# A recurrent block's output product: its rounded input waits for its own semaphore, and GpSimd forms two half rests

## The chip, the cores and the metric

The kernel runs on one core of one Trainium2 chip. The metric is the device time of one execution in microseconds (us), lower is better. Five engines work side by side, each in its own program order, and meet only through semaphores: TensorE (PE, matrix products), VectorE (DVE), ScalarE (ACT), GpSimd (POOL) and SyncE (SP, which here issues the loads of weights).

## What is computed

A stack of three layers over 256 tokens of width 1024, all in fp32: a mixer of four branches with a feed-forward layer, a gated linear recurrence (HGRN2) with a feed-forward layer, and a gated convolutional recurrence (RG-LRU) with a feed-forward layer. The change lies in the third, between the recurrence and its output product:

```python
def rglru_mixer(h, w_in, conv_w, conv_b, wa, ba, wx, bx, lam, w_out):
    proj = h @ w_in
    y, u = jnp.split(proj, [LRU_WIDTH], axis=-1)
    y = jax.nn.gelu(y.astype(jnp.float32))
    ...                                        # uc: a causal convolution of u; r, ig: two sigmoid gates of uc
    a = jnp.exp(log_a)
    b_in = jnp.sqrt(-jnp.expm1(2.0 * log_a)) * (ig * uc)
    _, hs = lax.associative_scan(combine, (a, b_in), axis=1)
    return (hs * y).astype(h.dtype) @ w_out    # the output product

x = x + mix
x = x + swiglu_2(rmsnorm_2(x, norm_ffn[l]), ffn_w_in[l], ffn_w_out[l])
```

## The kernel before

**Products in three passes.** Each fp32 matrix is split in two: a rounded part (`whi`, `ch`, `hh`: type fp32r) and a rest (`wlo`, `cl`, `hl`: the difference to the rounded part). A product is the sum of rounded by rounded (L527 for tokens as rows, L507 for columns), rounded by rest of the weights (L531, L510), and rest by rounded weights (L535, L515).

**Units of weights.** All weights come in units of 128 x 2048 elements through three slots (NS = 3). For each half of a unit: SP loads it into `raw` (L2207), ACT rounds it into `whi` (L981), DVE forms `wlo = raw - whi` (L1385). Where `on_pool` says so, GpSimd forms the rest of the unit's second half instead (L2006, the same subtraction). `light` (L301) is the list of units for which it does, so far most units of the three feed-forward layers. SP may load a half of unit j+3 once the rest of that half of unit j is set, and ACT may round it once TensorE has read unit j.

**The stretch of the change.** The recurrence's input units for y are `ly` 0 to 3, the units of its output weights `lo` 0 to 3 (each two k rows of 128 by 1024 columns, one k row to a half), and then come `g` 0, `u` 0, `g` 1 and so on of the last feed-forward layer. For the four pairs of channels n, called pair 0 to 3 here, the order written out by hand is:

- DVE scales y out of the PSUM bank (`y_of`, L1432), runs the scan (`scan`, L1933 and L1935), multiplies by the GELU (`gated`, L1942), and forms the rest `cl` (`gated_rest`, L1947), with the rests of weights (L1385) between. From 913.78 us on: y_of(2), gated(0), scan(2), gated_rest(0), gated(1), y_of(3), scan(3), gated_rest(1), rests of `lo` 1, gated(2), gated(3), gated_rest(2), gated_rest(3), rests of `lo` 2 and `lo` 3.
- ACT takes the GELU (L1330), rounds the gated output into `ch` (L1335, which raises `s_uch`), and rounds weights (L981) between: `lo` 1, gelu(2), ch of pair 0, ch of pair 1, gelu(3), `lo` 2, ch of pairs 2 and 3, `lo` 3.
- `cl` raises `s_hs`. DVE's `gated_rest(n)` waits for `s_uch`, so `cl` of a pair always comes after its `ch`.
- TensorE runs `add_product(("lo",), ...)` (L966): unit 0 for both column halves, then units 1, 2, 3 for the first half, then units 1, 2, 3 for the second. For each token half it runs two products of each pass: `ch` by `whi` (L527), `ch` by `wlo` (L531), `cl` by `whi` (L535). Before the first pass it waits for `hi(k)`, before the third for `lo(k)`. Both are `s_hs` so far, though the first two passes read only `ch`.
- GpSimd has nothing in this stretch before the change. Its program reaches the rests of a unit two units ahead, so its first instruction here waits only for `whi`.

```python
        def on_pool(j, h):
            return h == 1 and any(u0 <= j < u1 for u0, u1 in light)
...
                if 0 in parts:
                    for i, k in enumerate(ks):
                        tq.wait_ge(*hi_set(j, i // half_k))
                        tq.wait_ge(*hi(k))
```

Of the kernel before, what the change touches and what calls it, by code (L numbers as in the profile page):

```python
# [74 lines left out]
def build(nc, a):  # L75
    V, A, G, T, S = nc.vector, nc.scalar, nc.gpsimd, nc.tensor, nc.sync
    vq, aq, gq, tq, sq = Waits(V), Waits(A), Waits(G), Waits(T), Waits(S)
    with ExitStack() as root:
        def sem(name):
            return root.enter_context(nc.semaphore(name))  # L80

        def sbuf(ctx, name, shape, dt=f32):
            return ctx.enter_context(nc.sbuf_tensor(name, shape, dt))
# [73 lines left out]
        ch = sbuf(lr, "ch", [128, 8, 256], f32r)  # L157
        cl = sbuf(lr, "cl", [128, 8, 256], f32r)
# [51 lines left out]
        unit_at = {}  # L210
# [87 lines left out]
            raw_value.append(loads[j % NS])  # L298


        light = [(unit_at["g", f, 0] + 2, unit_at["g", f, 0] + 31) for f in range(3)]  # L301

        def on_pool(j, h):
            return h == 1 and any(u0 <= j < u1 for u0, u1 in light)
# [38 lines left out]
        s_pad, s_uch, s_gw = sem("pad_set"), sem("ch_set"), sem("gate_weights_landed")  # L343
# [3 lines left out]
        s_gel, s_gy, s_hs = sem("gelu_set"), sem("gated_set"), sem("lru_out_set")  # L347
# [7 lines left out]
        def turn(key, b, fills=1):  # L355
            fills_of[b] += fills
            turns[key] = (b, evacuations[b], fills_of[b])
            evacuations[b] += 1
            return b

        def free(key):
            b, n, _ = turns[key]
            return s_evac[b], n
# [120 lines left out]
        def halves_of(by_token):  # L484
            return [[(s, i) if by_token else (i, s) for i in range(2)] for s in range(2)]


        def tensor_program():
# [29 lines left out]
            def moving(out, j, t, xh, xl, ks, c0, n, hi, lo, first=True, last=True, parts=(0, 1, 2)):  # L518

                wh, wl = whole(whi, j), whole(wlo, j)  # L520
                r, c = slice(128 * t, 128 * t + 128), slice(c0, c0 + n)
                half_k = units[j][1] // 2
# [4 lines that stand above are left out]
                        tok = T.matmul(out, xh[:, k, r], wh[:, i, c], start=first and i == 0, stop=False)  # L527
                if 1 in parts:
                    for i, k in enumerate(ks):
                        tq.wait_ge(*lo_set(j, i // half_k))  # L530
                        tok = T.matmul(out, xh[:, k, r], wl[:, i, c], start=False, stop=False)  # L531
                if 2 in parts:
                    for i, k in enumerate(ks):
                        tq.wait_ge(*lo(k))
                        tok = T.matmul(out, xl[:, k, r], wh[:, i, c], start=False, stop=last and i == len(ks) - 1)  # L535
                return tok
# [31 lines left out]
            def transposes(c, e):  # L568

                for n in range(2):  # L570
                    b = turn(("tr", e, 2 * c + n), 4 + 2 * n + c)
                    for k in range(2):
                        for t in range(2):
                            col = 512 * c + 256 * n + 128 * k
                            tq.wait_ge(*hn_set(e, 2 * c + t))
                            tq.wait_ge(*free(("tr", e, 2 * c + n)))
                            tok = T.transpose(banks[b][:, 256 * k + 128 * t:256 * k + 128 * t + 128], hn[:, t, col:col + 128], ident[:, :])  # L577
                    tok.then_inc(s_full[b], 1)
# [27 lines left out]
            def add_product(key, n_units, xh, xl, hi, lo, e, by_token=False, inside_second=None, rests_last=False):  # L606

                halves = halves_of(by_token)

                def part(n, s, parts=(0, 1, 2), between=None):  # L610
                    j = unit_at[(*key, n)]
                    for t, c in halves[s]:
                        b, name = 4 + 2 * t + c, ("add", e, t, c)
                        if n == 0 and 0 in parts:
                            turn(name, b, n_units if b == 7 else 1)
                            tq.wait_ge(*free(name))
                        tok = moving(banks[b][:, :], j, t, xh, xl, [2 * n, 2 * n + 1], 512 * c, 512, hi, lo,
                                     first=n == 0, last=n == n_units - 1, parts=parts)
                        if 2 in parts and (b == 7 or n == n_units - 1):
                            tok.then_inc(s_full[b], 1)  # L620
                        if between is not None and (t, c) == halves[s][0]:
                            between()
                    if s == 1 and 2 in parts:
                        used[j, 0] = used[j, 1] = (s_full[7], turns["add", e, 1, 1][2] - n_units + n + 1)

                for n in range(n_units - 3):
                    for parts in ((0, 1), (2,)) if rests_last else ((0, 1, 2),):
                        part(n, 0, parts)
                        part(n, 1, parts)
                for n in range(n_units - 3, n_units):  # L630
                    part(n, 0, between=inside_second if n == n_units - 3 else None)
                for t, c in halves[0]:
                    turn(("sq", e, t, c), 4 + 2 * t + c, 0)
                for n in range(n_units - 3, n_units):
                    if n == n_units - 1 and e != 8:
                        transposes(0, e)
                    part(n, 1)
                for t, c in halves[1]:
                    turn(("sq", e, t, c), 4 + 2 * t + c, 0)
# [207 lines left out]
            def feed_forward(f, e, e2):  # L847
                project_pair([("g", f, 0), ("u", f, 0)], e)
                for j in range(1, 11):
                    project_columns(("g", f, j), e)  # L850
                    project_columns(("u", f, j), e)
                gh, gl = ffn[f][0:2]
                add_product(("down", f), 11, gh, gl, lambda k: (s_gh, 11 * f + k // 2 + 1), lambda k: (s_gl, 11 * f + k // 2 + 1),
                            e2, e2 == 8)
# [108 lines left out]
            project_columns(("ly", 2), 6)  # L963
            project_columns(("ly", 3), 6)
            rot_banks[0] = [0, 1, 2, 3]
            add_product(("lo",), 4, ch, cl, lambda k: (s_hs, k // 2 + 1), lambda k: (s_hs, k // 2 + 1), 7)  # L966
            feed_forward(2, 7, 8)


# [1226 lines left out]
        def sync_program():  # L2196
# [39 lines left out]
            sq.wait_ge(s_u, 16)  # L2236

        tensor_program()
        scalar_program()
        vector_program()  # L2240
# [30 lines left out]
```

## Time and profile before

| | |
|---|---|
| time, median of three runs | 1134.25 us (1134.21 to 1134.31) |
| span of the profiled execution | 1133.1 us |
| PE busy in it | 1119.1 us, 99% |
| DVE, ACT, POOL busy | 659.1, 571.9, 292.8 us |
| granted TensorE clock, mean | 0.999 of full speed |

The span runs from the first to the last instruction of the program, so 1.15 us of the median lie outside it. Times in the profile count from the span's start. A timeline row gives start, length, engine, line, operation, what is written from what, its shape, how often, and in brackets how long the engine had been idle before it and whose work ended that. On DVE and ACT an instruction's record begins up to 0.1 us before the one ahead of it ends, so a train of them is read by its starts.

### The profile page before, as it was taken

The numbers are of one execution on the slowest core, as the hardware profiler recorded it, in microseconds if no ns is written. First come the engines' busy times: TensorE is split into PE (matmuls) and PEld (weight loads), VectorE is DVE, ScalarE is ACT, GpSimd is POOL, SyncE is SP. The second block draws the span as 40 slices with busy tenths as digits, with TensorE's granted clock in tenths as the row PEclk, the third lists the DMA queues.
The fourth block names the chain that finished last, engine by engine and source line by source line (L and its number), as shares of the span: only waits on it lengthen the run. The fifth ranks groups of instructions, "written<-read, shape, count | busy, mean of one in ns | idle before, by whom it ended". The sixth has DMA issues, their size and how long they took to land.

```text
span 1133.1 us, 19238 instructions
## 1 busy us (share of the span) xinstructions
PE 1119.1 (99%) x8085; PEld 1040.8 (92%) x8085; DVE 659.1 (58%) x1052; ACT 571.9 (50%) x866; POOL 292.8 (26%) x193
## 2 busy tenths in 40 slices
PE   8999999999999999999999999999999999999997
PEld 7899989999989999889998889999889989999986
DVE  6755755677666454328897575443237897434324
ACT  6646555555445554336642544444335855544432
POOL 2023100000005445522411205444420003444440
PEclk9999999999999999999999999999999999999999
DMA  8689474544657656664545348665555255666551
GB/s 266 204 252 335 139 238 147 160 151 143 195 159 209 200 170 206 202 200 139 170 125 178 113 152 273 211 190 192 193 184 184 97 181 154 215 191 189 190 183 38
DMA packets 155088, 207.25 MB, mean 183 GB/s; under 512 B 9471, under 2 KB 128409, under 8 KB 155002
## 3 DMA queue, kind: packets, MB, share of 16 engines
q1 hardware_dynamic: 151274, 193.11, 54.4%
q0 software_dynamic: 3728, 12.92, 3.4%
q8 instruction: 64, 1.05, 0.4%
q14 instruction: 22, 0.18, 0.0%
HBM read 204.78 MB, written 4.24 MB: 184 GB/s over the span
## 4 chain that ended last, share of the span: by engine, by line
PE 84%; DVE 11%; ACT 3%; issue 1%; DMA 0%; POOL 0%; SPq 0%; DVEq 0%; ACTq 0%
PE bank L507 17%; PE bank L515 17%; PE bank L510 17%; PE bank L535 9%; PE bank L531 9%; PE bank L527 9%; DVE wlo L1385 4%; PE bank L886 1%; PE bank L802 1%; PE bank L812 1%; ACT whi L981 1%; DVE area L1533 1%; PE bank L577 1%; PE bank L824 1%; DVE uc L1533 0%
## 5 line engine op out<-in xcount | busy, mean ns | idle before, releaser
L1385 DVE TENSOR_TENSOR wlo<-raw,whi 128x1024 fp32r<-128x1024 f32 x275 | 336.5, 1251 | 231.4 <-ACT whi L981 230.6
L981 ACT ACTIVATE whi<-raw 128x1024 fp32r<-128x1024 f32 x362 | 360.4, 1044 | 107.3 <-PE bank L535 100.9
L2006 POOL TENSOR_TENSOR wlo<-raw,whi 128x1024 fp32r<-128x1024 f32 x87 | 222.7, 2560 | 250.9 <-ACT whi L981 250.9
L507 PE MATMUL bank<-hh,whi 128*128 128x256 f32 x1784 | 285.3, 281 | 0.0
L510 PE MATMUL bank<-hh,wlo 128*128 128x256 f32 x1784 | 281.3, 279 | 0.0
L515 PE MATMUL bank<-hl,whi 128*128 128x256 f32 x1784 | 281.3, 279 | 0.0
L507 PEld LDWEIGHTS bank<-hh,whi 128*128 128x128 f32 x1784 | 240.5, 188 | 3.4 <-issue 2.7
L510 PEld LDWEIGHTS bank<-hh,wlo 128*128 128x128 f32 x1784 | 239.8, 188 | 0.0
L515 PEld LDWEIGHTS bank<-hl,whi 128*128 128x128 f32 x1784 | 239.8, 188 | 0.0
L2013 POOL TENSOR_TENSOR st<-st,half 128x1 f32<-128x1 f32 x18 | 10.7, 604 | 331.4 <-DVE st L1402 302.2
L527 PE MATMUL bank<-whi,gh 128*128 128x512 f32 x264 | 81.6, 390 | 0.0
L531 PE MATMUL bank<-wlo,gh 128*128 128x512 f32 x264 | 81.3, 389 | 0.0
L535 PE MATMUL bank<-whi,gl 128*128 128x512 f32 x264 | 81.3, 389 | 0.0
L1211 ACT ACTIVATE sg<-sg 128x512 f32<-128x512 f32 x33 | 20.9, 633 | 94.2 <-DVE sg L1432 94.2
L1215 ACT ACTIVATE gh<-sg 128x512 fp32r<-128x512 f32 x33 | 20.8, 631 | 84.1 <-DVE sg L1765 84.1
L531 PEld LDWEIGHTS bank<-wlo,gh 128*128 128x128 f32 x264 | 49.6, 188 | 10.4
L535 PEld LDWEIGHTS bank<-whi,gl 128*128 128x128 f32 x264 | 49.6, 188 | 10.3
L527 PEld LDWEIGHTS bank<-whi,gh 128*128 128x128 f32 x264 | 49.2, 188 | 9.9
L1765 DVE TENSOR_TENSOR sg<-sg,bank 128x512 f32<-128x512 f32 x33 | 22.7, 688 | 55.6 <-PE bank L515 53.5
L1432 DVE TENSOR_TENSOR sg<-bank,bc_f 128x512 f32<-128x512 f32 x33 | 22.8, 690 | 45.4 <-PE bank L515 45.4
L1006 ACT ACTIVATE bank<-x_sb 128x512 f32<-128x512 f32 x26 | 15.6, 600 | 57.7 <-DVE x_sb L1454 29.9
L1767 DVE TENSOR_TENSOR gl<-sg,gh 128x512 fp32r<-128x512 f32 x33 | 30.7, 931 | 23.3 <-ACT gh L1215 23.3
(318 smaller groups left out, 1217.2 us busy)
## 6 DMA issues: line engine op xcount, KB each, us to landing
raw<-in_ffn_w_in SPq DMA_DIRECT2D x88, 512.0 KB, 3.8
raw<-in_w_in SPq DMA_DIRECT2D x72, 512.0 KB, 4.8
raw<-in_ffn_w_out SPq DMA_DIRECT2D x44, 512.0 KB, 3.2
raw<-in_hgrn_w_in SPq DMA_DIRECT2D x32, 512.0 KB, 4.4
raw<-in_w_ffn_gate SPq DMA_DIRECT2D x22, 512.0 KB, 4.6
raw<-in_w_ffn_up SPq DMA_DIRECT2D x22, 512.0 KB, 4.3
raw<-in_w_ffn_down SPq DMA_DIRECT2D x22, 512.0 KB, 3.4
raw<-in_w_branch SPq DMA_DIRECT2D x16, 512.0 KB, 4.3
```

Source lines behind the costliest of these rows:

```text
L507: T.matmul(out, wh[:, i, c], xh[:, k, :], start=first and (i, k) == pairs[0], stop=False)
L510: T.matmul(out, wl[:, i, c], xh[:, k, :], start=False, stop=False)
L515: t = T.matmul(out, wh[:, i, c], xl[:, k, :], start=False, stop=last and (i, k) == pairs[-1])
L527: tok = T.matmul(out, xh[:, k, r], wh[:, i, c], start=first and i == 0, stop=False)
L531: tok = T.matmul(out, xh[:, k, r], wl[:, i, c], start=False, stop=False)
L535: tok = T.matmul(out, xl[:, k, r], wh[:, i, c], start=False, stop=last and i == len(ks) - 1)
L981: A.activation(half_of(whi, j, h), half_of(raw, j, h), ACT.Copy).then_inc(s_hi[j % NS][h], 1)
L1385: V.tensor_tensor(half_of(wlo, j, h), half_of(raw, j, h), half_of(whi, j, h).bitcast(f32), ALU.subtract).then_inc(s_lo[j % NS][h], 1)
L1432: V.tensor_tensor(dst, two(bank_of("col", *key)[:, :]), bc[:, :].rearrange("p (o t) -> p o t", o=1).broadcast_to([128, 2, 256]), ALU.mult) ...
L1765: V.tensor_tensor(s, s, bank_of("col", "u", f, j)[:, :], ALU.mult).then_inc(evacuated("col", "u", f, j), 1)
L1767: V.tensor_tensor(gl[:, 2 * j:2 * j + 2, :], two(s), gh[:, 2 * j:2 * j + 2, :].bitcast(f32), ALU.subtract).then_inc(s_gl, 1)
L2006: G.tensor_tensor(half_of(wlo, j, 1), half_of(raw, j, 1), half_of(whi, j, 1).bitcast(f32), ALU.subtract).then_inc(s_lo[j % NS][1], 1)
```

## The change

It adds one stretch to `light`: units `lo` 1 and `lo` 2, whose second halves' rests GpSimd then forms instead of DVE. And it gives `add_product` of `lo` the semaphore of `ch`, `s_uch`, for the passes that read `ch`; the third pass keeps `s_hs`. Nothing is computed otherwise than before.

```diff
@@ -298,7 +298,7 @@
-        light = [(unit_at["g", f, 0] + 2, unit_at["g", f, 0] + 31) for f in range(3)]
+        light = [(unit_at["g", f, 0] + 2, unit_at["g", f, 0] + 31) for f in range(3)] + [(unit_at["lo", 1], unit_at["lo", 3])]
 
         def on_pool(j, h):
             return h == 1 and any(u0 <= j < u1 for u0, u1 in light)
@@ -963,7 +963,7 @@
             rot_banks[0] = [0, 1, 2, 3]
-            add_product(("lo",), 4, ch, cl, lambda k: (s_hs, k // 2 + 1), lambda k: (s_hs, k // 2 + 1), 7)
+            add_product(("lo",), 4, ch, cl, lambda k: (s_uch, k // 2 + 1), lambda k: (s_hs, k // 2 + 1), 7)
             feed_forward(2, 7, 8)
```

## Rows read from the trace of the kernel before

**Rows 1.** The page, busy time, share of span and instructions of each engine.

```profile
PE 1119.1 (99%) x8085; PEld 1040.8 (92%) x8085; DVE 659.1 (58%) x1052; ACT 571.9 (50%) x866; POOL 292.8 (26%) x193
```

**Rows 2.** Waits of PE: who for whom, us in total, times, longest.

```profile
PE bank L531 <- DVE wlo L1385: 1.6, 3, 0.7
...
PE bank L527 <- DVE cl L1947: 0.6, 1, 0.6
```

**Rows 3.** Windows: stretch, length, then busy us of PE, PEld, DVE, ACT, POOL.

```profile
942.50:1126.90 184.40, 184.40 (x1333) 173.88 (x1331) 77.29 (x86) 80.46 (x98) 74.94 (x32) 1.00 0.54 171
```

**Rows 4.** Timeline of PE in the output product.

```profile
917.70 0.70 PE L527 MATMUL bank<-whi,ch 128*128 128x512 f32 x2 [0.60 <-DVE cl L1947]
...
918.71 0.62 PE L535 MATMUL bank<-whi,cl 128*128 128x512 f32 x2
...
925.99 0.61 PE L527 MATMUL bank<-whi,ch 128*128 128x512 f32 x2
...
927.31 0.49 PE L531 MATMUL bank<-wlo,ch 128*128 128x512 f32 x1 [0.71 <-DVE wlo L1385]
...
928.44 0.50 PE L531 MATMUL bank<-wlo,ch 128*128 128x512 f32 x1 [0.64 <-DVE wlo L1385]
...
928.78 0.62 PE L535 MATMUL bank<-whi,cl 128*128 128x512 f32 x2
...
929.24 0.63 PE L527 MATMUL bank<-whi,ch 128*128 128x512 f32 x2
```

**Rows 5.** Timeline of DVE in the same stretch.

```profile
914.38 0.68 DVE L1942 TENSOR_TENSOR yg<-yg,ig 128x512 f32<-128x512 f32 x1
...
918.08 0.68 DVE L1432 TENSOR_TENSOR yg<-bank,bc_lr 128x512 f32<-128x512 f32 x1
...
921.17 1.22 DVE L1385 TENSOR_TENSOR wlo<-raw,whi 128x1024 fp32r<-128x1024 f32 x1
...
923.44 1.29 DVE L1942 TENSOR_TENSOR yg<-yg,ig 128x512 f32<-128x512 f32 x2
...
924.82 1.30 DVE L1947 TENSOR_TENSOR cl<-yg,ch 128x512 fp32r<-128x512 f32 x2
...
926.03 1.22 DVE L1385 TENSOR_TENSOR wlo<-raw,whi 128x1024 fp32r<-128x1024 f32 x1
...
927.17 1.22 DVE L1385 TENSOR_TENSOR wlo<-raw,whi 128x1024 fp32r<-128x1024 f32 x1
```

**Rows 6.** Timeline of ACT there: second halves of lo 1, lo 2, then ch.

```profile
913.12 1.05 ACT L981 ACTIVATE whi<-raw 128x1024 fp32r<-128x1024 f32 x1
...
920.28 1.05 ACT L981 ACTIVATE whi<-raw 128x1024 fp32r<-128x1024 f32 x1
...
924.15 1.24 ACT L1335 ACTIVATE ch<-yg 128x512 fp32r<-128x512 f32 x2 [2.83 <-DVE yg L1942]
```

**Rows 7.** Timelines of ACT, POOL and DVE in the first feed-forward layer.

```profile
416.99 1.04 ACT L981 ACTIVATE whi<-raw 128x1024 fp32r<-128x1024 f32 x1
...
418.11 2.40 POOL L2006 TENSOR_TENSOR wlo<-raw,whi 128x1024 fp32r<-128x1024 f32 x1 [3.11 <-ACT whi L981]
...
418.19 3.41 DVE L1385 TENSOR_TENSOR wlo<-raw,whi 128x1024 fp32r<-128x1024 f32 x1
...
349.59 5.21 POOL L2006 TENSOR_TENSOR wlo<-raw,whi 128x1024 fp32r<-128x1024 f32 x2 [4.43 <-ACT whi L981]
...
350.07 2.49 DVE L1767 TENSOR_TENSOR gl<-sg,gh 128x512 fp32r<-128x512 f32 x1 [0.77 <-ACT gh L1215]
352.48 3.41 DVE L1385 TENSOR_TENSOR wlo<-raw,whi 128x1024 fp32r<-128x1024 f32 x1
...
362.61 3.33 POOL L2006 TENSOR_TENSOR wlo<-raw,whi 128x1024 fp32r<-128x1024 f32 x1 [0.97 <-ACT whi L981]
...
364.38 0.69 DVE L1432 TENSOR_TENSOR sg<-bank,bc_f 128x512 f32<-128x512 f32 x1 [0.70 <-PE bank L515]
```

**Rows 8.** Loads from 915 to 945 us: count, size, median us to landing.

```profile
raw<-in_ffn_w_in SPq DMA_DIRECT2D x9, 512.0 KB, 4.7
```

## The prediction

> **What bounds the kernel now.** I read the busy times first: TensorE works 99% of the span [rows 1], so a change can matter only where TensorE waits or is made to wait. The list of its waits comes next. In the stretch of the change it has one wait of 0.60 us for `cl` and two, 0.71 and 0.64 us, for rests of weights [rows 2, 4]. The timeline gives them their place: 917.70, when the output product begins, and 927.31 and 928.44, the two `ch` by `wlo` products of unit `lo` 2 [rows 4]. From 942.50 to 1126.90 PE is busy for all of 184.40 us [rows 3], so what the output product gains or loses reaches the end in full. What sets the three waits is DVE: its train of instructions from gated(0) at 914.38 to the second rest of `lo` 2 at 927.17 has hardly a gap [rows 5]. So the question is what the change does to that train.
>
> **What GpSimd's instruction does to DVE.** The feed-forward layers have such pairs already. The rest on POOL took 2.40 us from 418.11 to 420.51; the same subtraction on DVE, queued at 418.19, lasted 3.41 us instead of 1.22, to 421.60, that is 1.09 us past POOL's end [rows 5, 7]. The 512-wide gl, which reads sg and gh and so nothing that POOL touches, stretched to 2.49 us and ended at 352.56, taking 2.40 us for the hold about 0.56 us after POOL's first of two [rows 7]. So a DVE instruction with two operands in SBUF stands still until POOL's is over. I count ten such starts inside a hold in the three layers, and none that went through. An instruction that reads a PSUM bank does go through: 0.69 us at 364.38, inside POOL's 362.61 to 365.94 [rows 7]. And POOL, when it comes second, waits for the running DVE instruction and then gets in ahead of DVE's next: its second rest ended at 354.80, 2.24 us after gl, and the DVE instruction queued behind gl waited for that (352.48, 3.41 us) [rows 7]. In DVE's train here, gated, scan, gated_rest and the rests have both operands in SBUF; only y_of reads a bank.
>
> **Part one, the wait for `ch`.** It removes up to 0.60 us at 917.70. By itself I price it at nothing: TensorE then reaches the rests of `lo` 2 0.60 us sooner, and DVE delivers them no sooner, so the waits at 927.31 and 928.44 grow by as much. The cover is those two waits; if part two took them away, the 0.60 us would count.
>
> **Part two, two rests to GpSimd.** It takes two DVE instructions of 1.14 us each (step from start to start, 927.17 less 926.03 [rows 5]) off the train and puts two POOL instructions of 2.40 us beside it.
>
> *First hold.* ACT's `whi` of the second half of `lo` 1 ends at 914.17 [rows 6]. POOL follows ACT by 0.08 us (418.03 to 418.11 [rows 7]), so it starts at 914.25, in front of gated(0) at 914.38 [rows 5]; at 418 a lead of 0.08 us was enough [rows 7]. It holds until 916.65. gated(0) ends 0.56 us later, at 917.21, where it ended at 915.06: 2.15 us late, and all behind it, `ch` and `cl` of pair 0 among them. TensorE's output product then begins at about 917.9 on `ch`, and waits again for `cl`, to about 919.75 against 918.71 [rows 4].
>
> *Second hold.* y_of(3) at 918.08 is in the train [rows 5], gelu(3) waits for it and ACT's `whi` of `lo` 2 stands behind gelu(3), so its end moves from 921.33 [rows 6] to 923.48 and POOL is ready at 923.56. DVE has begun the first rest of `lo` 1 at 923.32 (921.17 and 2.15 [rows 5]); it ends at 924.54, POOL gets in and is done 2.24 us later, at 926.78. gated(2), next on DVE with the second rest gone, ends at 927.34 instead of 924.12 (923.44 and 0.68 [rows 5]): 3.22 us late. As a sum: 2.15, plus 2.21 for the second hold, less 1.14 saved. `ch` of pair 2 follows on ACT and gated_rest(2) on DVE, with no slack in either direction (924.15, 924.82 [rows 5, 6]), so the first rest of `lo` 2 ends at 927.25 and 3.22, that is 930.47. The second comes from POOL, long since.
>
> *TensorE.* It stands before that rest from about 928.6. It resumed 0.05 us after DVE's end in the kernel before (928.39, 928.44), took 0.34 us to its next start (928.78), and 0.23 us for a step in flow (929.24 less 928.78, by two) [rows 4, 5]. So 930.52 for the first `wlo` product, 930.86 for the second, 931.09 for the `cl` product that stood at 928.78: **2.3 us late**.
>
> *What is late next: nothing.* `lo` 3's rests follow on DVE, ending at 931.6 and 932.75; TensorE wants them 0.46 us into `lo` 3, at about 933.4 and 933.6. SP's loads queue behind the rests: the first half of `g` 0 leaves at 924.5 instead of 922.4, that of `u` 0 at 930.5 instead of 927.3, and with 4.7 us to land [rows 8] they are there by 929.3 and 935.3, before ACT's turn at about 938.6 and 941.3 (which TensorE's reading of `lo` 1 and `lo` 2 sets). POOL's next work is the normaliser's power at 945 us. So 2.3 us stay, on the profiled span 1133.1 to 1135.4, on the median 1134.25 to **1136.5 us**.
>
> The GPSIMD Engine Reference of the Trainium skill (§ 2.1) puts the floor of a two-input instruction at about 2.5 cycles per element and § 1 the clock at 1.2 GHz; for 1024 elements that is an estimate of 2.13 us, against 2.40 us in the rows. By it each hold would be 0.27 us shorter and the loss about 1.8 us; the measured 2.40 us stands.
>
> **Bounds on what is not shown.** No row has POOL's rest beside gated or a scan, but gl is the same kind of instruction in the same shape. If DVE is first at 914.38, gated(0) goes through, POOL ends at 917.30 and scan(2) takes the blow: 2.2 us instead of 2.15, and 2.36 at the end. If POOL wins the second race too, the loss is 2.6. If POOL has to wait until DVE's queue leaves a gap, it gets in after gated(3), ends at 927.98, and the first rest of `lo` 2 ends at 930.28: 2.1 us. So 2.1 to 2.6 us, and I take 2.3, the row order.
>
> **Rivals.** *The train isn't held up (not slower).* If the stall were of the weights' subtraction alone, or POOL's rest slid beside the recurrence, DVE's train would be 1.14 us early from 922.3 on. TensorE would begin at 917.10, find `ch` ready, want the first rest of `lo` 2 at 925.84 and get it at 926.17 (926.12 and 0.05); the `cl` product would stand at 926.75 against 928.78, a gain of 2.0 us: 1132.2 us, within 0.2% by a little. It decides at 914.38: does gated(0) end at 915.06? Against it speaks gl, held without sharing a tile with POOL [rows 7].
>
> *One hold only.* If the first is as worked out and the second finds DVE between instructions of little weight, gated(2) is 1.0 us late (2.15 less 1.14), the first rest of `lo` 2 ends at 928.25, TensorE's `cl` product stands at 928.9, and the loss is 0.1 us: 1134.4 us. It needs POOL at 923.56 to miss the train; against it, DVE has no gap there [rows 5].
>
> The Trainium skill, SBUF — State Buffer (§ SBUF: two separate sides), has the pair of ports that DVE and GpSimd share as an exclusive lock, held for the whole instruction by the one that starts first. By that rule DVE couldn't keep it over several instructions, which speaks against a late entry of POOL; the row at 352.48 agrees.
>
> **How the numbers follow.** Holds as worked out, with their orders: 0.88, at 2.1 to 2.6 us. One hold: 0.05. No hold: 0.05. Something not seen, such as a longer restart of TensorE: 0.02. This kernel's measurement can tell about 0.2%, 2.27 us, from no change, and my forecast lies just beyond that line, so the main case is split: of 0.88 I give 0.50 to a loss over 2.27 us (2.3, 2.36 and 2.6 lie there, if barely) and 0.38 to less. One hold goes to the same; of no hold, 0.02 to faster. Faster 0.02, same 0.46, slower 0.52. The range takes the bounds 2.1 and 2.6 with 0.5 us on either side for the estimates: 1135.8 to 1137.4 us.
>
> **What would show it.** In the changed profile, POOL's two rests near 914.25 and 924.5; gated(0) and gated(2) of 2.8 and 2.9 us instead of 0.68; TensorE's waits of about 0.9 us for `ch`, 0.6 for `cl`, 1.0 for `ch` of pair 2 and 1.9 for the rest of `lo` 2; the first `cl` product of `lo` 2 at 931.1; no wait of TensorE from 945 us on. A gated(0) of 0.7 us would prove the prediction wrong at its first step, a rest of `lo` 2 before 929.5 at its second.

## The result and the profile after

| | before | changed |
|---|---|---|
| time, median | 1134.25 us (1134.09 to 1134.76, 7 runs) | 1136.98 us (1136.43 to 1138.79, 7 runs) |
| ratio to before | | 1.0028 [1.0019, 1.0037] |
| span of the profiled execution | 1133.1 us | 1135.6 us |
| PE, DVE, POOL busy in it | 1119.1, 659.1, 292.8 us | 1118.9, 660.9, 297.7 us |

The change loses 2.7 us by the medians, a quotient of 1.0024. The seven times aren't one heap: four lie at 1136.43 to 1136.98 us and three at 1138.44 to 1138.79 us. The three draw the mean, 1137.55 us, above the median, and the ratio of 1.0028 is nearer to the quotient of the means. The profiled execution, 1136.83 us, is of the lower group. The upper one is the subject of the last experiments.

GpSimd's two rests in the changed kernel's timeline of POOL:

```profile
914.49 2.40 POOL L2006 TENSOR_TENSOR wlo<-raw,whi 128x1024 fp32r<-128x1024 f32 x1 [52.92 <-ACT whi L981]
923.77 3.24 POOL L2006 TENSOR_TENSOR wlo<-raw,whi 128x1024 fp32r<-128x1024 f32 x1 [6.88 <-ACT whi L981]
```

DVE's train beside them, in the timeline of DVE:

```profile
914.02 0.69 DVE L1432 TENSOR_TENSOR yg<-bank,bc_lr 128x512 f32<-128x512 f32 x1
914.62 2.81 DVE L1942 TENSOR_TENSOR yg<-yg,ig 128x512 f32<-128x512 f32 x1
...
923.54 1.22 DVE L1385 TENSOR_TENSOR wlo<-raw,whi 128x1024 fp32r<-128x1024 f32 x1
924.68 2.89 DVE L1942 TENSOR_TENSOR yg<-yg,ig 128x512 f32<-128x512 f32 x1
...
929.48 1.22 DVE L1385 TENSOR_TENSOR wlo<-raw,whi 128x1024 fp32r<-128x1024 f32 x1
```

The two 512-wide gated products, 0.68 us before [rows 5], take 2.81 and 2.89 us: each lasts until about 0.55 us after POOL's end (914.62 and 2.81 is 917.43, POOL ends at 916.89; 927.57 against 927.01). In the second race DVE was first, with the rest at 923.54; it ended at 924.76, and POOL 2.25 us after it.

TensorE's waits in its timeline, where [rows 4] had 0.60, 0.71 and 0.64 us:

```profile
918.25 0.70 PE L527 MATMUL bank<-whi,ch 128*128 128x512 f32 x2 [1.10 <-ACT ch L1335]
...
919.99 0.73 PE L535 MATMUL bank<-whi,cl 128*128 128x512 f32 x2 [0.58 <-DVE cl L1947]
...
928.37 0.70 PE L527 MATMUL bank<-whi,ch 128*128 128x512 f32 x2 [0.83 <-ACT ch L1335]
930.75 0.73 PE L531 MATMUL bank<-wlo,ch 128*128 128x512 f32 x2 [1.67 <-DVE wlo L1385]
931.32 0.63 PE L535 MATMUL bank<-whi,cl 128*128 128x512 f32 x2
```

And the rest of the kernel, in windows (stretch, length, busy us of PE, PEld, DVE, ACT, POOL, then the granted clock, DMA share and GB/s):

```profile
926.90:930.60 3.70, 1.34 (x5) 0.48 (x3) 3.61 (x5) 3.00 (x4) 0.12 (x1) 1.00 0.64 224
...
945.20:1129.00 183.80, 183.80 (x1331) 173.59 (x1330) 77.12 (x85) 80.02 (x97) 74.95 (x32) 1.00 0.54 171
```

PE never stands from 945.20 on, so what is lost by 931 us reaches the end. The first `cl` product of `lo` 2 starts at 931.32 against 928.78 [rows 4], 2.54 us later. Of these, 0.24 us are an offset that stood on DVE already ahead of GpSimd's first rest (y_of(2) at 914.02 against 913.78 us in the kernel before); an offset of about 0.3 us is there from the first layer on, far ahead of the change. So 2.30 us are the change's.

### The profile page after: what moved, and what is told of

Same layout as the page of the kernel before. It is cut to its first block, busy times and chain, and to the rows that moved or that the text cites. A ratio compares the mean times of both kernels' runs of the same rounds, so it can differ in the third digit from the quotient of the medians.

```text
span 1135.6 us, 19238 instructions
## 1 busy us (share of the span) xinstructions
PE 1118.9 (99%) x8085; PEld 1040.2 (92%) x8085; DVE 660.9 (58%) x1050; ACT 571.7 (50%) x866; POOL 297.7 (26%) x195
## 4 chain that ended last, share of the span: by engine, by line
PE 83%; DVE 11%; ACT 3%; issue 1%; DMA 1%; POOL 0%; SPq 0%; DVEq 0%; ACTq 0%
PE bank L507 17%; PE bank L515 17%; PE bank L510 17%; PE bank L531 9%; PE bank L535 9%; PE bank L527 9%; DVE wlo L1385 3%; PE bank L886 1%; PE bank L802 1%; ACT whi L981 1%; PE bank L812 1%; DVE area L1533 1%; DMA raw<-in_w_in 1%; PE bank L824 1%; PE bank L577 1%
## 5 line engine op out<-in xcount | busy, mean ns | idle before, releaser
L2006 POOL TENSOR_TENSOR wlo<-raw,whi 128x1024 fp32r<-128x1024 f32 x89 | 228.3, 2565 | 310.7 <-ACT whi L981 310.7
```

Source lines behind the costliest of these rows:

```text
L2006: G.tensor_tensor(half_of(wlo, j, 1), half_of(raw, j, 1), half_of(whi, j, 1).bitcast(f32), ALU.subtract).then_inc(s_lo[j % NS][1], 1)
```

## The experiments

Two theories were put to the test first: that the loss comes from DVE standing during POOL's instruction, and, against it, that it comes from the wait or from the order of the rests. Later a third question came up, the upper group. The kernel before ran beside each: its medians were 1134.20 to 1134.35 us.

**One part alone.** First only the wait:

```diff
-            add_product(("lo",), 4, ch, cl, lambda k: (s_hs, k // 2 + 1), lambda k: (s_hs, k // 2 + 1), 7)
+            add_product(("lo",), 4, ch, cl, lambda k: (s_uch, k // 2 + 1), lambda k: (s_hs, k // 2 + 1), 7)
```

> Only the wait for the rounded output's own semaphore; no rest goes to GpSimd. Theory of the hold (GpSimd's subtraction keeps VectorE's two-input instructions standing, VectorE's train sets the end): no change, 1134.2 us within 0.2 us. TensorE begins the output product 0.6 us sooner (wait of 0.60 us gone) and waits 0.6 us longer before the first rest of unit 2. Rival (TensorE's early start and its extra waits are what costs): 1135 to 1136 us, TensorE's products after a wait slower than 0.34 us to the next start, or a granted clock under 1.00 behind them.

Measured: 1134.46 us (11 runs, 1134.15 to 1135.81), ratio 1.0003 [0.9994, 1.0012]. Its timeline of PE, and the row of PE's waits for rests (us in total, times, longest):

```profile
917.00 0.62 PE L527 MATMUL bank<-whi,ch 128*128 128x512 f32 x2
...
923.87 0.50 PE L531 MATMUL bank<-wlo,ch 128*128 128x512 f32 x1 [0.45 <-DVE wlo L1385]
927.60 0.49 PE L531 MATMUL bank<-wlo,ch 128*128 128x512 f32 x1 [0.90 <-DVE wlo L1385]
928.73 0.50 PE L531 MATMUL bank<-wlo,ch 128*128 128x512 f32 x1 [0.64 <-DVE wlo L1385]
```

```profile
PE bank L531 <- DVE wlo L1385: 2.2, 4, 0.9
```

The output product begins 0.70 us earlier than in [rows 4], without a wait, and the gain is gone by 928.73. Its waits for rests add up to 2.2 us, as much as the 1.6 us for rests and the 0.6 us for `cl` of [rows 2] together: a wait of 0.45 us for the rest of `lo` 1 is new, and the first for `lo` 2 is longer, 0.90 us against 0.71. The 0.26 us by which its median lies above the kernel before beside it is within the noise. Part one is worth nothing by itself, as priced.

Then only the rests on GpSimd:

```diff
-        light = [(unit_at["g", f, 0] + 2, unit_at["g", f, 0] + 31) for f in range(3)]
+        light = [(unit_at["g", f, 0] + 2, unit_at["g", f, 0] + 31) for f in range(3)] + [(unit_at["lo", 1], unit_at["lo", 3])]
```

> Only the two rests to GpSimd; the first two passes wait for the rests of the output, as before. Theory of the hold: the same loss as the whole change, 2.3 us (1136.5 us), since TensorE stands before the first rest of unit 2 whenever it began; gated of pair 0 and of pair 2 held 2.8 to 2.9 us. Rival (the early start costs): no more than 0.5 us of loss here. Rival (an extra loss outside the output product, seen in the runs of the change near 1138.6 us, belongs to the hold): some runs near 1138.5 here too, and none with the wait alone.

Measured: 1136.63 us (11 runs, 1136.37 to 1138.13), ratio 1.0022 [1.0014, 1.0031]. The loss of the lower group is all in part two. One of the 11 times, 1138.13 us, stands apart; the profiled execution was that one, and it shows something new. Its timeline and windows of PE:

```profile
920.61 1.19 PE L527 MATMUL bank<-whi,ch 128*128 128x512 f32 x2 [2.96 <-DVE cl L1947]
921.60 1.05 PE L531 MATMUL bank<-wlo,ch 128*128 128x512 f32 x2
922.46 1.05 PE L535 MATMUL bank<-whi,cl 128*128 128x512 f32 x2
...
926.69 0.63 PE L531 MATMUL bank<-wlo,ch 128*128 128x512 f32 x2
```

```profile
923.00:926.00 3.00, 3.00 (x9) 2.32 (x8) 3.00 (x4) 1.24 (x2) 1.69 (x1) 0.50 0.00 0
```

After one wait of 2.96 us (the changed kernel has it in two pieces, 1.10 and 0.58 us) the granted clock is 0.50, that is 1.2 of 2.4 GHz, and two products take 0.86 us from start to start instead of 0.46 until about 926.7. About half of what sets this execution apart is an offset (y_of(2) stands at 914.56 against 913.78 us in the kernel before); by the first `cl` product of `lo` 2, at 932.62 us, about 0.8 us beyond the hold's 2.3 are left for the low clock.

**The changed kernel again**, unaltered, to see whether its two groups come back.

> The changed kernel once more, for the spread of its runs: the seven timed so far lie at 1136.4 to 1137.0 and at 1138.4 to 1138.8 us, the kernel before at 1134.1 to 1134.8. Theory: 1136.5 us is the stall of 2.3 us alone, and the upper group is a second thing; if it is a lower granted clock behind TensorE's long waits, a profile from the upper group shows windows under 1.00 after 930 us and an output product as in the first profile. If it is another order at the port, the output product itself ends 2 us later.

Measured: four runs at 1136.44 to 1136.60 us, four at 1138.25 to 1138.46 us; median 1137.42 us, ratio 1.0028 [1.0018, 1.0038]. The profile, of a run at 1136.60 us, has a low clock too, in another place:

```profile
919.60:924.00 4.40, 4.28 (x12) 3.36 (x13) 4.37 (x8) 3.13 (x4) 0.50 (x1) 0.61 0.00 0
```

It follows the waits of 1.14 and 0.57 us at 917.98 and 919.72, and it costs nothing: TensorE reaches the rest of `lo` 2 later, and waits 1.12 us for it instead of 1.67 us. A clock that falls ahead of a wait is paid out of the wait. The upper group therefore needs a fall behind the last wait.

**One hold at a time**, with the new wait in both; the edits are against the changed kernel. The first, `lo` 1 alone:

```diff
-        light = [(unit_at["g", f, 0] + 2, unit_at["g", f, 0] + 31) for f in range(3)] + [(unit_at["lo", 1], unit_at["lo", 3])]
+        light = [(unit_at["g", f, 0] + 2, unit_at["g", f, 0] + 31) for f in range(3)] + [(unit_at["lo", 1], unit_at["lo", 2])]
```

> The change with only unit 1's second rest on GpSimd; unit 2's stays on VectorE. Theory of the hold, from the train of the kernel before: one hold of 2.15 us less one rest of 1.14 us, so the second rest of unit 2 ends at 929.40 instead of 928.39 and TensorE's first product of the third pass of unit 2 stands at 929.8: 1.0 us late, 1135.3 us. TensorE's waits stay under 1 us each, so if long waits bring the lower clock, no run lies 1.5 us above the rest. Rival (a hold costs nothing once TensorE's own waits are hidden): 1134.3 us.

Measured: 1135.36 us (10 runs, 1135.12 to 1135.91), ratio 1.0009 [0.9999, 1.0018]. DVE in it:

```profile
914.22 2.81 DVE L1942 TENSOR_TENSOR yg<-yg,ig 128x512 f32<-128x512 f32 x1
...
924.26 1.28 DVE L1942 TENSOR_TENSOR yg<-yg,ig 128x512 f32<-128x512 f32 x2
```

gated(0) pays 2.15 us for the hold, the train gets back 1.14 us for the rest it needn't form, and 1.0 us arrives at the end. The interval of the ratio just takes in 1, so this rests on the trace: the first `cl` product of `lo` 2 stands at 929.61 us against 928.78, and y_of(2) at 913.62 against 913.78, which makes 0.99 us. No execution lies 1.5 us above the rest.

The second, `lo` 2 alone:

```diff
-        light = [(unit_at["g", f, 0] + 2, unit_at["g", f, 0] + 31) for f in range(3)] + [(unit_at["lo", 1], unit_at["lo", 3])]
+        light = [(unit_at["g", f, 0] + 2, unit_at["g", f, 0] + 31) for f in range(3)] + [(unit_at["lo", 2], unit_at["lo", 3])]
```

> The change with only unit 2's second rest on GpSimd; unit 1's stays on VectorE. Theory of the hold: GpSimd is ready at 921.4, gets in behind unit 1's first rest at 922.4 and keeps unit 1's second rest standing to 925.7 (3.4 us instead of 1.2). TensorE waits 2.5 us for that and 1.1 us for the first rest of unit 2 at 929.5; the first product of the third pass of unit 2 stands at 930.1: 1.3 us late, 1135.5 us. If a long wait brings the lower clock, some or all runs show it behind the 2.5 us wait, where the 1.1 us wait can take up part of it.

Measured: 1135.81 us (10 runs, 1135.39 to 1136.15), ratio 1.0012 [1.0003, 1.0021]. DVE, then PE, then PE's window:

```profile
921.02 4.52 DVE L1385 TENSOR_TENSOR wlo<-raw,whi 128x1024 fp32r<-128x1024 f32 x2
```

```profile
925.59 0.79 PE L531 MATMUL bank<-wlo,ch 128*128 128x512 f32 x1 [2.49 <-DVE wlo L1385]
```

```profile
926.00:931.00 5.00, 5.00 (x17) 3.97 (x17) 4.91 (x7) 3.13 (x4) 0.00 (x0) 0.70 0.44 121
```

Here POOL lands on the two rests of `lo` 1, which take 4.52 us together instead of 2.35. Behind a single wait of 2.49 us the granted clock is low, as in the run with the rests alone. The time is 0.3 us over the estimate of the hold.

**The hold without the rests' move.** The kernel before, with two additional GpSimd subtractions of the same shape at the same places, into a part of the tile `th` that nothing reads any more (the wait for `s_tr` is for its last reader); DVE still forms all rests. This adds work and saves none:

```diff
             use(("ly", 3))
+            gq.wait_ge(s_tr, 4)
+            for n in (1, 2):
+                gq.wait_ge(*hi_set(unit_at["lo", n], 1))
+                gq.wait_ge(*own_p.mark(G.tensor_tensor(th[:, 0:4, :], th[:, 0:4, :], th[:, 4:8, :], ALU.subtract)))
             add_product(("lo",), 4, 7)
```

> The kernel before, unchanged in all its rests and waits, with two subtractions more on GpSimd, 128x1024 each, on a tile that nothing reads any more, at the moments at which the change has its two rests (after the rounding of unit 1's and of unit 2's second half). It measures the hold by itself, without the two rests taken off VectorE. Theory: gated of pair 0 held 2.15 us, then unit 1's second rest held (3.3 to 3.4 us instead of 1.2), the train 4.35 us late, 1138.6 us; more by up to 2 us where the clock falls behind a long wait of TensorE. Rival (the loss is in the change's own order of rests, loads or waits, not at the port): 1134.3 us.

Measured: 1138.98 us (4 runs, 1138.56 to 1140.19), ratio 1.0042 [1.0028, 1.0055]. POOL, then DVE, in the profile (the run at 1140.19 us):

```profile
914.20 2.40 POOL L2194 TENSOR_TENSOR th<-th 128x1024 f32<-128x1024 f32 x1 [52.99 <-ACT whi L981]
```

```profile
914.27 2.88 DVE L1942 TENSOR_TENSOR yg<-yg,ig 128x512 f32<-128x512 f32 x1
...
923.25 4.56 DVE L1385 TENSOR_TENSOR wlo<-raw,whi 128x1024 fp32r<-128x1024 f32 x2
```

POOL's instruction shares no tile with gated(0), and gated(0) stands as before. So the loss is the stall of DVE by GpSimd's instruction, not the weights' data or the order of the rests. No semaphore ties the two either: the engines do not meet only through semaphores, as the section on the chip has it. The lowest time, 1138.56 us, is 4.2 us over the 1134.35 us of the kernel before beside it: two holds of 2.15 and 2.21 us with nothing saved. The profiled execution lies 1.6 us higher, and has a low clock in two places. Its windows, and PE ahead of the second:

```profile
917.00:926.00 9.00, 6.21 (x20) 5.01 (x21) 8.93 (x13) 3.76 (x5) 2.45 (x1) 0.81 0.11 43
934.00:936.00 2.00, 2.00 (x6) 1.61 (x5) 0.95 (x1) 0.00 (x0) 0.00 (x0) 0.50 0.95 308
```

```profile
931.60 0.50 PE L531 MATMUL bank<-wlo,ch 128*128 128x512 f32 x1 [0.89 <-DVE wlo L1385]
932.74 0.50 PE L531 MATMUL bank<-wlo,ch 128*128 128x512 f32 x1 [0.64 <-DVE wlo L1385]
```

The first fall is behind a wait of 2.79 us and ahead of others. The second is behind two waits of 0.89 and 0.64 us, hardly longer than the 0.71 and 0.64 us of [rows 4], and no wait follows that could take it up.

**Does the upper group come from the clock?** Three more single executions of the changed kernel were profiled, to catch one of it.

> The changed kernel, one look for its upper group of times. If the time is 1138.2 or more: theory, an output product like the first profile's up to unit 2's first rest (its first third-pass product 2.2 to 2.4 us late against the kernel before but for the start), and behind it a granted clock of 0.50 for about 4 us, products a step of 0.43 us apart, 1.9 us lost. If it is below 1137: clock at 1.00 from 930 us on.

> As for the first look: either the time is 1138.2 or more and the granted clock is 0.50 for about 4 us behind unit 2's first rest, or it is below 1137 and the clock is 1.00 there.

> As for the first look: either the time is 1138.2 or more and the granted clock is 0.50 for about 4 us behind unit 2's first rest, or it is below 1137 and the clock is 1.00 there.

Measured: 1138.55, 1136.48 and 1136.54 us; the first is of the upper group. PE in it:

```profile
930.86 0.73 PE L531 MATMUL bank<-wlo,ch 128*128 128x512 f32 x2 [1.67 <-DVE wlo L1385]
931.43 0.78 PE L535 MATMUL bank<-whi,cl 128*128 128x512 f32 x2
932.01 1.05 PE L527 MATMUL bank<-whi,ch 128*128 128x512 f32 x2
932.86 1.05 PE L531 MATMUL bank<-wlo,ch 128*128 128x512 f32 x2
...
935.30 0.62 PE L531 MATMUL bank<-wlo,ch 128*128 128x512 f32 x2
```

```profile
926.90:930.60 3.70, 1.50 (x6) 0.63 (x4) 3.60 (x5) 2.89 (x4) 0.23 (x1) 1.00 0.67 233
...
932.00:934.00 2.00, 2.00 (x6) 1.60 (x5) 1.08 (x1) 0.00 (x0) 0.00 (x0) 0.50 0.96 305
```

The same product in the profile of the changed kernel, 1136.83 us:

```profile
932.24 0.62 PE L531 MATMUL bank<-wlo,ch 128*128 128x512 f32 x2
...
933.61 0.62 PE L531 MATMUL bank<-wlo,ch 128*128 128x512 f32 x2
```

Up to the first `cl` product the two executions agree within 0.11 us (931.43 and 931.32), with the same wait of 1.67 us. Then one runs at clock 0.50 in 932 to 934 us and the other at 1.00. The product that starts at 935.30 us in the one starts at 933.61 us in the other: 1.58 us lost beyond the 0.11. From there to the end the distance grows by only 0.02 us, to 1.71.

Then the waits were filled. The kernel is the changed one, with 8, 4, 6 and 13 more products of 256 columns in front of the four waits, into a bank that is free there and that nobody reads:

```diff
...
+                        if key == ("lo",) and (t, c) == halves[0][0] and n in (0, 2):
+                            for p, count in enumerate(((8, 0, 4), (6, 13, 0))[n // 2]):
+                                keep_busy(count)
+                                tok = moving(banks[b][:, :], j, t, xh, xl, [2 * n, 2 * n + 1], 512 * c, 512, hi, lo,
+                                             first=n == 0, last=n == n_units - 1, parts=(p,))
...
```

> The changed kernel with TensorE's four new waits filled: 8, 4, 6 and 13 extra products of 128x256 (0.117 us each) on operands at hand, into a bank that nobody reads, before the first pass of unit 0, before its third pass, before unit 2 and before its second pass. VectorE and GpSimd do as in the change. Theory (the upper group of the change's runs, 1138.2 to 1138.8, is the granted clock falling behind TensorE's long waits at unit 2): all runs at 1136.4 to 1136.9, none above 1137.5, granted clock 1.00 from 917 to 935 us. Rival (the upper group is another order at the port, or the loads): about half of the runs at 1138 and above, as in the change.

Measured: 1136.66 us (11 runs, 1136.42 to 1137.22), ratio 1.0019 [1.0011, 1.0028]. Its window:

```profile
917.00:935.00 18.00, 17.64 (x90) 14.59 (x89) 16.05 (x20) 6.89 (x9) 3.24 (x1) 1.00 0.41 139
```

The hold's 2.3 us stay and the upper group is gone, in none of 11 executions where the changed kernel has it in 8 of 18 (three of the first seven, four of the next eight, one of the three single ones). In the profiled execution TensorE is busy for 17.64 of 18.00 us and the granted clock is 1.00. The changed kernel itself did not run beside this one; the run of the second hold alone and that of the additional subtractions did, and both show a low clock in their profiles.

**The other way to help TensorE.** If DVE's train is the bound, the rests should be wanted later, not formed elsewhere. Here `add_product` runs units 0 and 1 of `lo`, not 0 alone, for both column halves before unit 2; all rests are DVE's, and the wait is the new one:

```diff
-                for n in range(n_units - 3):
+                both = n_units - 3 if both is None else both
+                for n in range(both):
...
-                for n in range(n_units - 3, n_units):
+                for n in range(both, n_units):
...
+            add_product(("lo",), 4, ch, cl, lambda k: (s_uch, k // 2 + 1), lambda k: (s_hs, k // 2 + 1), 7, both=2)
```

> No rest goes to GpSimd. The wait for the rounded output's own semaphore, and TensorE takes units 0 and 1 for both column halves before unit 2, instead of unit 0 alone: 12 products of 0.227 us, 2.7 us, are put in front of unit 2, so that VectorE's train has that much longer for unit 2's rests. Theory (the train of VectorE is the bound and TensorE's waits at unit 2 cost 1.9 us): those two waits go, the 0.60 us wait goes and now counts; a wait of some 0.3 us for the second rest of unit 1 stays, and the normalised rows are ready (1.9 us after the first half's last product) before the transposes ask (2.7 us after it): 2.0 to 2.3 us faster, 1132.0 us. Rival (the early waits are hidden anyway, or the shorter cover makes the transposes wait): 1134.0 to 1134.6 us with a new wait of TensorE for hn.

Measured: 1132.67 us (11 runs, 1132.46 to 1133.18), ratio 0.9986 [0.9977, 0.9995]. Behind unit 2 TensorE is 1.9 us ahead of the kernel before (the first transposes start at 936.88 against 938.78 us), and 1.36 us at the end (span 1131.7 against 1133.1 us). So the forecast of 1132.0 us was 0.7 us too low, and the rival's wait for `hn` came in part. The 0.5 us go at the second transposes of the normalised sum:

```profile
936.79 3.50 DVE L1386 TENSOR_TENSOR wlo<-raw,whi 128x1024 fp32r<-128x1024 f32 x3 [0.54 <-ACT whi L982]
...
942.59 1.29 DVE L1398 TENSOR_TENSOR hn<-x_sb,wrow 128x512 f32<-128x512 f32 x2
```

```profile
943.33 0.33 PE L577 MATMUL bank<-ident,hn 128*128 128x128 f32 x1
943.93 0.98 PE L577 MATMUL bank<-ident,hn 128*128 128x128 f32 x7 [0.27 <-DVE hn L1398]
```

Three rests of the next units stand on DVE in front of the sums that `hn` needs. So they were brought forward: ACT and DVE split both halves of `g` 0 ahead of the first half's sums, the same two lines in either program:

```diff
                     before_last()
+                if key == ("lo",):
+                    split_to(unit_at[(*key, n_units - 1)] + 1)
                 for s in range(2):
```

> No rest on GpSimd. The wait for the rounded output's own semaphore, units 0 and 1 for both column halves before unit 2, and ScalarE and VectorE form the two halves of the next layer's first unit before the first column half's sums instead of behind them. In the run without that last step TensorE kept 1.9 us at unit 2 and lost 0.5 us again at the second pair of transposes, since three rests of the next layer stood on VectorE in front of what they wait for. Theory: with two of the three moved up into VectorE's idle 2 us, that wait goes: 1132.1 us. Rival (the rests moved up delay the first column half's sums and the first transposes): 1132.7 us or more, with a wait of TensorE for hn before the first transposes.

Measured: 1132.16 us (11 runs, 1132.01 to 1132.58), ratio 0.9981 [0.9972, 0.9990]. The rests and the transposes:

```profile
938.39 1.23 DVE L1388 TENSOR_TENSOR wlo<-raw,whi 128x1024 fp32r<-128x1024 f32 x1 [1.98 <-ACT whi L982]
...
941.93 1.29 DVE L1400 TENSOR_TENSOR hn<-x_sb,wrow 128x512 f32<-128x512 f32 x2
```

```profile
943.48 1.04 PE L577 MATMUL bank<-ident,hn 128*128 128x128 f32 x8
```

One rest is left at that place, and the eight transposes run through (span 1131.3 us). This version is 2.1 us under the kernel before and 4.8 us under the changed one.

## Why the prediction was right, and where it failed

**The first hold: right.** Forecast: POOL at 914.25, gated(0) ends at 917.21. Less the offset of 0.24 us the profile has POOL at 914.25 and the end at 917.19. The run with this hold alone puts 1.0 us on the time, 2.15 less 1.14.

**The order at the second hold: right.** POOL done at 926.78, gated(2) at 927.34, the first rest of `lo` 2 at 930.47 were forecast; less the offset they are at 926.77, 927.33 and 930.46. POOL got in after one DVE instruction, so the bound of 2.1 us for a late entry and the rival of one hold fall, and with gated(0) at 2.81 us the rival without a hold. That the stall doesn't hang on shared data was settled by the run with the unrelated subtractions. The Trainium skill, SBUF — State Buffer (§ SBUF: two separate sides), calls the pair of ports an exclusive lock for a whole instruction; the 2.81 us agree.

**GpSimd's duration: the row was right.** The first hold took 2.40 us, as in [rows 7]. The estimate of 2.13 us from the Trainium skill, GPSIMD Engine Reference (§ 2.1, § 1), which calls the figure a floor, was too short.

**Part one: right for the hold.** Nothing by itself (1134.46 us), and nothing beside the rests as far as the lower group goes: 1136.63 us without it, a median of 1136.55 us over the changed kernel's ten lower runs. But without it only one of 11 executions stood apart, against 8 of 18 with it, and that one had its long wait at the start of the output product and not at unit 2. So the new wait may make the upper group more frequent; the runs are too few to show it.

**TensorE's waits: nearly right.** Forecast about 0.9, 0.6, 1.0 and 1.9 us; measured 1.10, 0.58, 0.83 and 1.67. Their sum, 4.4 against 4.18 us, moves nothing, since what matters is the rest's end. The first `cl` product was forecast at 931.1 and stands at 931.08 less the offset. Nothing waits after 945 us.

**The step that failed: what TensorE does once it resumes.** The sum put 0.34 us to its next start and then 0.23 us for a step in flow, taken from rows behind waits of 0.6 to 0.7 us [rows 4], and held that for all executions; "a longer restart of TensorE" had 0.02. In fact the change makes the last two waits about 0.8 and 1.67 us, with only 1.34 and 1.50 us of products in the 3.70 us around them in the two executions shown, and behind them the granted clock was 1.00 in some executions and 0.50 in others. In the one caught, the first step after the wait is as forecast, 0.57 us to the `cl` product, and the following ones take 0.43 us each instead of 0.23, until 1.58 us are lost. Without that loss the time is the 1136.55 us of the ten lower runs, 2.30 us over 1134.25, as the hold was priced. The eight upper ones have a median of 1138.45 us, 1.9 us more, of which the one traced shows 1.6. That the other seven fell for the same cause wasn't traced; that no run with filled waits joins them speaks for it.

**The sign and the line of 0.2%.** The text put the loss of 2.3 us just beyond the line of 2.27 us, and gave slower 0.52; but the time that it ends on, 1136.5 us, is a loss of 2.25 us and lies just short of it. A fair reading of the hold alone was "on the line", and the run with the filled waits is on it: 1.0019, with an interval that has 1.002 inside. What draws the changed kernel's ratio up to 1.0028 is the upper group, and so the clock, which the working left out. It should have stood as a rival of its own, about 2 us above the forecast. The range, 1135.8 to 1137.4 us, took in the first median, 1136.98 us, and just missed that of the repeat, 1137.42 us; the upper group lies outside it. That the first median lies inside is luck: four of its seven executions were of the lower group, and with one more in the upper it would have been 1138.4 us.

## What to carry to other kernels

Before handing a two-operand subtraction to GpSimd, look whether VectorE has a gap of that length: in a train without gaps 2.40 us on GpSimd cost 2.2 us and saved 1.14. (That such a gap makes it free was not tried here.) If a train of VectorE sets the time, make its consumer want the results later; here that gave 1.5 us, and 2.1 us with two of the next rests brought forward. When a change lengthens waits of TensorE, price the products behind the last wait at half clock as a case of its own; it was 1.6 us in the one traced here.

## What the runs showed of the hardware

GpSimd's instruction, once it waits for a running VectorE instruction, got in ahead of VectorE's next in the changed kernel and in each variant of it profiled here with a second hold: POOL took 3.18 to 3.24 us instead of 2.40 there, the excess being the wait.

The granted clock behind a given pattern of waits isn't the same in each execution. With nearly the same waits, 0.79 and 1.67 us in one and 0.83 and 1.67 us in another, it was 0.50 in the first and 1.00 in the second. Behind single waits of 2.49 us (the second hold alone), 2.79 us (the two additional subtractions) and 2.96 us (the rests alone) it was low in each of the three profiles: 0.70 over 926 to 931 us, 0.81 over 917 to 926 us, 0.50 over 923 to 926 us. The Trainium skill, TensorE: Matmul & The Clock Gate (§ HAM oscillation — how this bites in real kernels), tells of a clock that falls in the gaps between bursts of products; these rows agree in kind, but the waits here are shorter than those it tells of. Why nearly equal waits end at either level is open.

The second fall in the run with the additional subtractions, behind 0.89 and 0.64 us, says that it doesn't take the changed kernel's waits. Single executions of the kernel before (1135.80 us) and of the wait alone (1135.81 us) lie about 1.4 us above their medians and may be of the same kind; neither was traced.

A low clock ahead of a wait was free (919.60 to 924.00 us at 0.61, in a run at 1136.60 us); the same behind the last wait cost 1.6 us.
